# Hybrid decoder step with a sparse expert stage: the router's activations in other buffers, one expert matrix loaded during the output product, first refills in quarters and halves

## What is computed

```python
def hier_moe(h, rg_w, rg_b, re_w, re_b, w_gate, w_up, w_down):
    ...
    lg = tf @ rg_w.astype(jnp.float32) + rg_b.astype(jnp.float32)
    ...
    top_v, top_i = lax.top_k(le, TOP_K_INNER)
    ...
    for e in range(N_EXPERTS):
        hid = jax.nn.silu(t @ w_gate[e].astype(t.dtype)) * (t @ w_up[e].astype(t.dtype))
        acc = acc + combine[:, e:e + 1] * (hid @ w_down[e].astype(t.dtype))
```

## Time and profile before

| | us |
|---|---|
| median of 3 executions | 797.75 (797.67 to 797.92) |
| the profiled execution, its own time | 798.58 |
| span of that execution, first to last instruction | 796.9 |
| TensorE busy in the span | 763.7 (96%) |
| VectorE, ScalarE, GpSimd busy | 272.6, 156.8, 139.7 |
| bytes moved by DMA | 249.58 MB, mean 313 GB/s |

### The profile page before, as it was taken

One profiled execution on the slowest core, in us unless ns is written; L12 is line 12 of the kernel. 1 busy time (PEld: TensorE's weight loads), 2 busy tenths in 40 slices (PEclk: granted clock), 3 DMA queues, 4 the chain that ended last, 5 costly groups with the idle time before them and its releaser, 6 DMA issues.

```text
span 796.9 us, 8780 instructions
## 1 busy us (share of the span) xinstructions
PE 763.7 (96%) x3510; PEld 365.7 (46%) x3510; DVE 272.6 (34%) x626; ACT 156.8 (20%) x312; POOL 139.7 (18%) x168
## 2 busy tenths in 40 slices
PE   5999999999999999899999999999999999899896
PEld 4777677767853335544333333333333333233332
DVE  2059999996646522521011101100110111010003
ACT  3310121225632002200121011111111210110122
POOL 2079899712002000100000000000000000000000
PEclk9999999999999999789999999999999999999999
DMA  9894200040839686899999999999999999999992
GB/s 271 305 378 168 106 21 0 1 114 5 288 133 296 212 302 287 300 379 403 427 426 425 428 427 426 426 428 424 428 425 429 427 425 429 426 424 430 425 381 71
DMA packets 51400, 249.58 MB, mean 313 GB/s; under 512 B 6982, under 2 KB 24422, under 8 KB 38671
## 3 DMA queue, kind: packets, MB, share of 16 engines
q1 hardware_dynamic: 45604, 243.41, 76.4%
q10 hardware_dynamic: 3227, 2.80, 1.3%
q0 software_dynamic: 2528, 2.79, 1.2%
HBM read 246.87 MB, written 8.61 MB: 321 GB/s over the span
## 4 chain that ended last, share of the span: by engine, by line
PE 93%; DVE 2%; DMA 2%; issue 2%; ACT 1%; SPq 0%; DVEq 0%; POOLq 0%
PE bank L1221 28%; PE bank L807 20%; PE bank L1244 14%; PE bank L1085 9%; PE bank L1269 9%; PE bank L1204 2%; DMA ring<-in_w_in 1%; PE bank L1233 1%; PE bank L1074 1%; PE bank L1043 1%; PE bank L909 1%; PE bank L1222 1%; DVE region_a L1648 1%; PE bank L1056 0%; PE bank L920 0%
## 5 line engine op out<-in xcount | busy, mean ns | idle before, releaser
L807 PE MATMUL bank<-region_a,ring 128*128 128x320 f32 x576 | 159.7, 438 | 2.1 <-DMA ring<-in_w_in 2.1
L1648 DVE TENSOR_TENSOR region_a<-region_a,bank 64x512 f32<-64x512 f32 (+1 forms) x33 | 22.4, 680 | 376.9 <-ACT region_a L1575 376.9
L1222 PE MATMUL bank<-ring,zz 128*64 128x512 f32 x320 | 142.0, 598 | 0.0
L807 PEld LDWEIGHTS bank<-region_a,ring 128*128 128x128 f32 x576 | 110.1, 193 | 48.6 <-issue 5.1
L1221 PE MATMUL bank<-ring,zz 128*64 128x512 f32 x288 | 127.3, 595 | 1.0 <-issue 1.0
L1649 DVE SCALAR_TENSOR_TENSOR bank<-region_a,par,bank 128x256 f32<-128x256 f32 x232 | 91.2, 480 | 0.0
L760 POOL DMA_INDIRECT region_a<-hn_scratch,region_a x16 | 15.9, 996 | 373.2 <-PE bank L1204 358.4
L1269 PE MATMUL bank<-zz,masks 128*128 128x512 f32 (+1 forms) x192 | 77.2, 603 | 0.7 <-ACT zz L1581 0.7
L1221 PEld LDWEIGHTS bank<-ring,zz 128*64 128x64 f32 x288 | 38.1, 137 | 80.7 <-issue 80.0
L1085 PE MATMUL bank<-ring,x_v_y 128*128 128x512 f32 (+1 forms) x192 | 74.0, 605 | 0.0
L1575 ACT ACTIVATE region_a<-bank 64x512 f32<-64x512 f32 x32 | 18.9, 590 | 270.1 <-PE bank L1222 270.1
(11 more groups left out here) (320 smaller groups left out, 785.8 us busy)
## 6 DMA issues: line engine op xcount, KB each, us to landing
ring<-in_expert_w_up SPq DMA_DIRECT2D x20, 2048.0 KB, 24.6
ring<-in_expert_w_gate SPq DMA_DIRECT2D x17, 2048.0 KB, 29.9
ring<-in_expert_w_down SPq DMA_DIRECT2D x16, 2048.0 KB, 34.7
ring<-in_w_in SPq DMA_DIRECT2D x9, 2048.0 KB, 20.1
x_v_y<-in_expert_w_down SPq DMA_DIRECT2D x6, 2048.0 KB, 33.2
x_v_y<-in_expert_w_gate SPq DMA_DIRECT2D x5, 2048.0 KB, 34.2
ring<-in_w_out SPq DMA_DIRECT2D x4, 2048.0 KB, 7.8
xcx<-in_expert_w_gate SPq DMA_DIRECT2D x4, 2048.0 KB, 31.2
```

The source lines that it names most:

```text
L807: ins = pe.matmul(pt[0:m, 0:T], w[:, k, :], ht[:, k, :], start=k == 0, stop=k == KD - 1)
L1222: ins = pe.matmul(to[CAP:P, :], x[:, k, :], wu[:, FE * k:FE * k + FE], **st)
L1648: tt_ = lambda out, a, b, op: dve.tensor_tensor(out, a, b, op)
```

## The change

It touches four things.

1. `h2t`, the router's transposed rows, is split over two other buffers: the first four k in the first 1280 columns of `zz`, the other four at the end of the router's small buffers in `region_a`, over the place of `gat` and part of `tokno`. So the first 4096 columns of `region_a` are free once `y_done` is given, and matrix 8 is issued early: right behind matrix 1, ahead of the state writes of c = 2 and on.
2. Since `gat` and `tokno` are covered, GpSimd writes both only after `lg2`, and VectorE waits for `tokno` ahead of its first `places`. `square2` writes into the rows `hn`, which `normed` overwrites right after.
3. Matrix 9 is loaded whole after `hn_out`; nothing waits for `gath_begun` any more. Matrix 10 still waits for `kept`.
4. Matrices 11 and 12 come in quarters, after k = 1, 3 and 5 and the end of expert 0's gate and up, matrices 13 and 14 in halves, after k = 3 and the end of expert 1's.

```diff
-        h2t = ra[:, 0:KD * T].rearrange("p (k t) -> p k t", k=KD)
...
+        h2t = [t.rearrange("p (k t) -> p k t", k=4) for t in (zf[:, 0:4 * T], ra[:, at[0] - 4 * T:at[0]])]
...
-            if j == n_slot - 2:
-                eng.wait_ge(S("tenth_half"), 16)
             if j in (n_slot, n_slot + 1):
-                eng.wait_ge(S("first_halves"), 32)
+                eng.wait_ge(S("first_parts"), 96)
+            if j in (n_slot + 2, n_slot + 3):
+                eng.wait_ge(S("second_parts"), 32)
...
                     load_expert(1)
+                    sp_.wait_ge(S("y_done"), 1)
+                    load_expert(n_slot - 3)
...
-            sp_.wait_ge(filled, J[("lg2",)] + 1)
-            load_expert(n_slot - 3)
...
             sp_.wait_ge(S("hn_out"), 48)
-            load_half(n_slot - 2, 0, S("tenth_half"))
-            sp_.wait_ge(S("gath_begun"), 1)
-            load_half(n_slot - 2, 1, expert_in[n_slot - 2])
+            load_expert(n_slot - 2)
             sp_.wait_ge(S("kept"), 1)
             load_expert(n_slot - 1)
 
-            sp_.wait_ge(S("gu_half"), 1)
-            for j in (n_slot, n_slot + 1):
-                load_half(j, 0, S("first_halves"))
+            for h in range(3):
+                sp_.wait_ge(S("gu_part"), h + 1)
+                for j in (n_slot, n_slot + 1):
+                    load_part(j, h, 4, S("first_parts"))
             sp_.wait_ge(S("gu_done"), 1)
             for j in (n_slot, n_slot + 1):
-                load_half(j, 1, expert_in[j % n_slot])
-            for j in range(n_slot + 2, len(EXPERT)):
+                load_part(j, 3, 4, expert_in[j % n_slot])
+            sp_.wait_ge(S("gu_part"), 4)
+            for j in (n_slot + 2, n_slot + 3):
+                load_part(j, 0, 2, S("second_parts"))
+            sp_.wait_ge(S("gu_done"), 2)
+            for j in (n_slot + 2, n_slot + 3):
+                load_part(j, 1, 2, expert_in[j % n_slot])
+            for j in range(n_slot + 4, len(EXPERT)):
...
-            pool.iota(tokno, [[1, T]], base=0, channel_multiplier=0, allow_small_or_imprecise_dtypes=True)
...
-            pool.wait_ge(filled, J[("outs",)] + 1)
+            pool.wait_ge(filled, J[("lg2",)] + 1)
+            pool.iota(tokno, [[1, T]], base=0, channel_multiplier=0, allow_small_or_imprecise_dtypes=True)\
+                .then_inc(S("tokno"), 1)
             link(pool.memset(gat, 0.0))
...
-                act.activation(zf[0:n, 0:D], xt[0:n, r, :], ACT.Square, accum_out=ssq[0:n, r:r + 1])\
+                act.activation(hn[0:n, r, :], xt[0:n, r, :], ACT.Square, accum_out=ssq[0:n, r:r + 1])\
```

More of the change, by code:

```diff
@@ L552, in _, with load_part @@
                 load_expert(m + 2)
-            sp_.wait_ge(filled, J[("lg2",)] + 1)
-            load_expert(n_slot - 3)
-            def load_half(j, h, sem):
-                part = slice(UNIT // 2 * h, UNIT // 2 * h + UNIT // 2)
+            def load_part(j, h, n, sem):
+                part = slice(UNIT // n * h, UNIT // n * h + UNIT // n)
                 sp_.dma_start(e_slot[j % n_slot][:, part], expert_src(*EXPERT[j])[:, part]).then_inc(sem, 16)
             sp_.wait_ge(S("hn_out"), 48)
-            load_half(n_slot - 2, 0, S("tenth_half"))
-            sp_.wait_ge(S("gath_begun"), 1)
-            load_half(n_slot - 2, 1, expert_in[n_slot - 2])
+            load_expert(n_slot - 2)
             sp_.wait_ge(S("kept"), 1)
             load_expert(n_slot - 1)
-            sp_.wait_ge(S("gu_half"), 1)
-            for j in (n_slot, n_slot + 1):
-                load_half(j, 0, S("first_halves"))
+            for h in range(3):
+                sp_.wait_ge(S("gu_part"), h + 1)
+                for j in (n_slot, n_slot + 1):
+                    load_part(j, h, 4, S("first_parts"))
             sp_.wait_ge(S("gu_done"), 1)
             for j in (n_slot, n_slot + 1):
-                load_half(j, 1, expert_in[j % n_slot])
-            for j in range(n_slot + 2, len(EXPERT)):
+                load_part(j, 3, 4, expert_in[j % n_slot])
[6 more added lines that the diff above has]
+            for j in range(n_slot + 4, len(EXPERT)):
                 m, e = EXPERT[j - n_slot]
@@ L1129, in logits @@
                 for k in range(KD):
-                    ins = pe.matmul(pt[0:n, 36 * r:36 * r + 36], h2t[:, k, t0:t0 + n], wr[:, k, :],
+                    ins = pe.matmul(pt[0:n, 36 * r:36 * r + 36], h2t[k // 4][:, k % 4, t0:t0 + n], wr[:, k, :],
                                     start=k == 0, stop=k == KD - 1)
@@ L1214, in carry_wait, with gate_up @@
                 pe.transpose(b_t[:, 0:P], ident[:, :], ident[:, :])
-            def gate_up(to, x, wg, wu, first=False):
+            def gate_up(to, x, wg, wu, parts=(), first=False):
                 for k in range(KD):
@@ L1222, in gate_up @@
                     ins = pe.matmul(to[CAP:P, :], x[:, k, :], wu[:, FE * k:FE * k + FE], **st)
-                    if first and k == 3:
-                        ins.then_inc(S("gu_half"), 1)
+                    if k in parts:
+                        ins.then_inc(S("gu_part"), 1)
                 return ins
@@ L1301, in _ @@
                     pe.wait_ge(S("xgt"), 2 * i + 2 if e else 1)
-                    gate_up(to, xgt[:, :, own_half[e % 2]], gate, up, first=e == 0).then_inc(S("gu_done"), 1)
+                    gate_up(to, xgt[:, :, own_half[e % 2]], gate, up, {0: (1, 3, 5), 1: (3,)}.get(e, ()),
+                            first=e == 0).then_inc(S("gu_done"), 1)
                 more = i + 1 < NE // 2
@@ L1876, in h2_gain @@
                     v = pt[:, :].rearrange("p (k t) -> p k t", k=4)[:, :, 0:n]
-                    tt_(h2t[:, 4 * q:4 * q + 4, toks(r)], v,
+                    tt_(h2t[q][:, :, toks(r)], v,
                         bc(lnffn[:, 4 * q:4 * q + 4].unsqueeze(2), [P, 4, n]), ALU.mult).then_inc(free["dve"], 1)
@@ L2016, in places @@
                 return dve.tensor_scalar(back[b], tokno, tok, w, ALU.is_equal, ALU.mult)
+            dve.wait_ge(S("tokno"), 1)
             for i in range(NE // 2):
```

## The result

The changed kernel is slower. Its median is 803.91 us (801.04 to 805.26, four runs), that of the kernel before beside it 797.71. The ratio is 1.0071, with a 95% interval of 1.0052 to 1.0090. A second comparison, on another chip, gave 802.60 against 797.50, ratio 1.0061 (1.0044 to 1.0078). The forecast was 796.7 us with a range of 795.2 to 799.4, so the time lies above it.

What follows compares the result with a forecast made beforehand. DMA's stream of matrices, slower than TensorE by some 2.1 us a pair, was taken to bound the kernel. Gain and gather delay, -1.5 + 0.4 = -1.1 us, took the median from 797.75 to 796.7 us; range 795.2 to 799.4.

Steps and rivals of the forecast that it cites:

- The bound: Stream of matrices by DMA limits TensorE; an advance of up to 9.6 us shortens the run one for one.
- Part 1 and 2 together: Early matrix 8 plus quarters and halves empty the queue ahead of matrix 15: 1.5 us gained, all from matrix 8.
- matrix 15's landing at 8.4 us: Check on the gain: matrix 15 lands about 8.4 us after its issue; at 9.9 the first term is wrong.
- whole matrix: Rival: backlog, not matrix 15's issue, sets the stream, so all 4.9 us come; 792.9 us, chance 0.05.
- Part 3: Matrix 9 whole, matrix 10 ahead of the first gather: the cost, start of the expert stage slips 0.4 us.
- x: Delay of the first gather by matrix 10: taken as 0.8 us, between 0 and 2.1, far end 7.6.
- The clock's share: At the expert stage's start the clock rise keeps its time, so 0.4 of the 0.8 us delay comes back.
- The slower rival: First gather held up, clock stays low: start slips 3.1 us, 799.3 us; chance 0.22, half of it above 799.35.
- point of decision: Slip of the expert stage's start from which the change loses: 1.5 us.
- The sentence on the Trainium skill: Each gathered row waits for one 0.6 us packet of matrix 10: gather delay 0.6 to 1.2, time 796.5 to 796.9.
- Part 4: Moved buffers, `tokno`, `gat`, `square2`: GpSimd's later work is covered by over 7 us of waiting; cost 0.
- The waits ahead of gate and up: Check: TensorE's waits for matrices late in the run should sum to about 6.8 us in place of 7.9.

Runs made afterwards that it cites:

- e2: Kernel before with only the wait for the first gather's issue, ahead of matrix 9's second half, taken out; 804.44 us, ratio 1.0080.
- e1: Changed kernel with the wait for the first gather's issue (the hold) put back, now ahead of matrix 10; 797.23 us, ratio 0.9997.
- e5: Changed kernel with matrix 10 held until the first gather has landed; 797.58 us, ratio 0.9995.
- e9: e1 with matrices 15 to 18 in halves too, first halves after the fourth step of experts 2 and 3; 797.21 us, ratio 0.9994.
- e4: e1 with the refills of matrices 11 to 14 as before: 11 and 12 in halves, 13 and 14 whole; 798.07 us, ratio 1.0002.
- e10: Kernel before with only the quarters of matrices 11 and 12 and halves of 13 and 14 added; 798.11 us, ratio 1.0004.
- e3: e1 with matrix 8 issued late again, directly ahead of a whole matrix 9; 802.63 us, ratio 1.0056.
- e8: Changed kernel with matrix 9 also waiting for `kept`, so two whole matrices go right ahead of the first gather; 804.80 us, one run.
- e7: Changed kernel with half of matrix 10 issued ahead of the first gather and half after the gather's issue; 797.61 us, one run.
- e6: Changed kernel with matrix 10, still ahead of the first gather, in four parts with packets of 4 KB; 801.93 us, one run.

## Why the prediction was wrong, by its own steps

**The bound** held. From 374 to 640 us both engines are full at 427 GB/s as before. What moved the stream moved the end: in e2, whose refills are the old ones, matrix 15's issue came 6.68 us later and the last wait was over 6.81 us later. That an advance shortens the run one for one is not shown: e1, e5 and e9 have their last wait over 1.2 to 2.5 us sooner than the kernel before, and their ratios are 0.9997, 0.9995 and 0.9994.

**Part 1 and 2 together, -1.5 us,** held in size up to the last wait: 1.97 and 1.44 us were recovered in the two profiles of the changed kernel. In the time, for which it was forecast, it isn't there: with the hold the median lies 0.2 us below that of the kernel before, by the interval between 1.4 below and 1.0 above. The check that I had named, matrix 15's landing at 8.4 us, gave 8.7 and 9.7, so that view alone scatters by 1 us and is a poor test of a term of 1.5. The attribution failed. I gave all of it to the early matrix 8 and nothing to the pieces; in e4's profile matrix 8 alone brings 0.1, and in e10's the pieces alone bring 0.1. The rows of the table speak for the pieces as what recovers the time: all that recover it have them. Whether they need the early matrix 8 is open: e10 says yes, while e3, with matrix 8 late and the gather late, recovers 2.2. That matrix 15's issue anchors the stream was borne out with the old refills; with the pieces, e9 issued half of it 4.0 us sooner without an effect on the last wait. The rival "whole matrix" is refuted by e4. I had also counted eight more issues on SyncE, where matrices 11 to 14 have six more (twelve in place of six); nothing hangs on it.

**Part 3 is the step that failed:** x was taken as 0.8 us and is 4.68 (8.40 against 3.72). My bounds were the second gather (2.1) and, as the far end, the third (7.6), and I chose below even the nearer one, because "matrix 10 only begins then". That reason was backwards. A gather that is nearly through when the matrix's bytes begin is safe, as in e1; one that is issued 0.11 us behind the matrix has all of it beside it. The starting point was also wrong in kind: I priced a delay by how full the queue was, and left out the count of the gather's packets and the late first one. With that step the slip of matrix 15's issue, 0.4 us in the forecast, came to 5.78.

**The clock's share** had the wrong sign. I let 0.4 us of the delay come back, because the rise would keep its time at about 342.75. It didn't: TensorE was busy 1.01 us of 6.50 while it waited, and the clock was still at 0.50 from 345.5 to 348. That cost 1.10 us more (in the second profile 0.7), not 0.4 less. The slower rival had this mechanism (gather late, idle for longer, clock low), with a price of 3.1 us, and its point of decision, a slip of 1.5 us, was passed by far. Its sentence on a gather as long as the third gave "about 804". I had put 0.22 on that rival, with half of it above 799.35; on the rows I had, the second gather's 2.1 already passed the point of decision, so the slower side deserved more than it got.

**The sentence on the Trainium skill** (DMA: Bandwidth & Descriptors, section on queues, rings and completion order) cited the rule that a DMA engine goes round its queues packet by packet. The rule holds in this case: 27 packets against 27 in one window of e8. I had worked it out for one packet of each gathered row in bounds, so for one or two turns, which gave 0.6 to 1.2 us. The rows out of bounds take turns as well: in e8 that is 1.09 us for the issue, 3.2 or more to the first packet and nine turns of 0.61 us, together 9.8 us, where 11.41 were measured; the remaining 1.6 us are not accounted for. In the changed kernel matrix 10 is through before the last turns, so it is 8.40. I had also written that the third gather's 11.3 us speak against the rule. They don't: that gather, beside a queue full to the end, has all nine turns to wait for, like e8's 11.41. The kernel before shows it from 366 to 367:

```profile
q1 hardware_dynamic: 23, 0.38, 88.6%
...
q0 software_dynamic: 23, 0.00, 1.3%
```

**Part 4** held. GpSimd's moved work is done at 325.41, over 8 us ahead of the gather:

```profile
324.11 0.40 POOL L753 IOTA region_a<- 128x320 f32 x1 [60.47 <-PE bank L1136]
324.46 0.95 POOL L755 MEMSET region_a<- 128x1024 f32 x1
333.79 1.09 POOL L766 DMA_INDIRECT region_a<-hn_scratch,region_a  x1 [8.38 <-DVE region_a L1961]
```

The early matrix 8 pushed matrix 2 from 271.71 to 273.68, as foreseen, and nobody waited.

**The waits ahead of gate and up** were to sum to 6.8 us and came to 6.1 and 6.8. I put that down to TensorE coming later to a stream that had recovered part of the delay, not to a gain: with the hold, where TensorE starts early, they sum to 8.3 (e1). TensorE's pair still takes 27.3 us (SyncE's issues of the same load at 502.87 and 530.19).

## What to carry to other kernels

A small DMA on the critical path, beside a stream of large packets, cost here one turn for each of its packets on a DMA engine, and its first packet came late as well. So count its packets, those of rows out of bounds among them, not its bytes. Hold back not only the issue right ahead of it but whatever would still be flowing while it runs. When the stream of weights is the bound, ask of every loosened wait whether the delay that it allows lands ahead of the point where the stream itself is released; there it was paid in full (e2) or all but 1 to 2 us of it (after, e8).

## What the runs showed of the hardware that I had not expected

- The first gather lands 2.9 to 3.7 us after its issue with a quiet queue, 6.8 beside packets of 4 KB or behind half a matrix, 8.4 and 8.6 beside one matrix, 10.3 beside one and a half (e2), 11.4 beside two (e8), and 9.4 beside the end of matrix 9 and matrix 10 issued behind it (e3).
- On a quiet queue its first packet moves 0.6 us after GpSimd's issue has ended (e1, e4, e5, e9, e10, before). With a load issued right ahead of it this is 2.7 to 3.8 us (e7, e6, after, e8, e2), with an earlier matrix still under way and nothing just issued 1.9 (e3). Why is open: no run separates the reading of the index from the queue.
- Packets of 4 bytes take the same turn as those of 4 KB (e8, 343 to 344: 27 of the gather, 0.00 MB, against 27 of 16 KB, 0.44 MB; from 340 to 341, with rows of 4 KB among them, 22 against 23).
- When TensorE resumes after the gather, the clock is at 1.2 GHz, and its rise is bound to no moment in the run: products have their short duration from 342.77 in the kernel before (transposes from 339.10), 343.93 in e7 (from 340.46) and 348.37 in the changed one (from 342.33).
- A wait of 2.0 us late in the run was followed by a stretch at 1.2 GHz in e1 and e3, which made the rest 1.8 us longer, and by none in before, e4, e8 and e9.
